# A mixture-of-experts decoder layer on one core: expert weights in six transfers of 2 MB per job instead of twelve of 1 MB

## What is computed

```python
logits = jnp.dot(hf, w_router) + b_router
top_v, top_e = lax.top_k(logits, TOP_K)            # TOP_K = 4
top_w = jax.nn.softmax(top_v, axis=-1)
...
def expert_block(args):                            # 128 rows of one expert
    xb, e = args
    gu = xb @ w_gate_up[e] + b_gate_up[e]          # w_gate_up[e]: 1024 x 2048
    gate = jnp.minimum(gu[:, 0::2], SWIGLU_LIMIT)
    up = jnp.clip(gu[:, 1::2], -SWIGLU_LIMIT, SWIGLU_LIMIT)
    act = (up + 1.0) * gate * jax.nn.sigmoid(SWIGLU_ALPHA * gate)
    return act @ w_down[e] + b_down[e]             # w_down[e]: 1024 x 1024
```

## Time and profile before

| | before |
|---|---|
| median of 3 runs | 2044.56 us |
| the profiled execution | 2048.57 us, of which the span 2046.5 us |
| TensorE (PE) busy | 1911.9 us, 93% of the span |
| VectorE (DVE) busy | 1455.7 us, 71% |
| ScalarE (ACT) busy | 1105.6 us, 54% |
| GpSimd (POOL) busy | 363.6 us, 18% |
| moved by DMA | 500.21 MB in 247399 packets |
| loads of gate-up / down pieces | 262 / 128, 1024.0 KB each |

### The profile page before, as it was taken

How to read it: one execution, slowest core, us unless ns; L and a number is a source line. 1 busy time by engine, 2 the same in 40 slices (tenths; PEclk the granted TensorE clock), 3 DMA queues, 4 the chain that set the end, 5 groups by cost and what they waited for, 6 DMA issues and landing times.

```text
span 2046.5 us, 27803 instructions
## 1 busy us (share of the span) xinstructions
PE 1911.9 (93%) x9552; PEld 1487.8 (73%) x9552; DVE 1455.7 (71%) x1677; ACT 1105.6 (54%) x1203; POOL 363.6 (18%) x260
## 2 busy tenths in 40 slices
PE   6899899975899986599999999999999999999998
PEld 2444699943756886488888888888888888888884
DVE  4517544344522454599999999999999999999995
ACT  2014222215541221277777777777777777777771
POOL 2000333302000000022222131222212121222211
PEclk9999999977799997599999999999999999999998
DMA  9820000003003221599999999999999999999996
GB/s 349 314 74 1 0 1 2 1 1 149 1 1 123 83 83 55 198 368 364 371 366 372 366 371 369 363 371 368 367 366 371 370 369 369 371 369 364 371 364 245
DMA packets 247399, 500.21 MB, mean 244 GB/s; under 512 B 14730, under 2 KB 16839, under 8 KB 246131
## 3 DMA queue, kind: packets, MB, share of 16 engines
q1 hardware_dynamic: 235108, 480.87, 64.8%
q0 software_dynamic: 9648, 17.32, 2.3%
q10 hardware_dynamic: 2592, 1.31, 0.2%
HBM read 495.76 MB, written 21.51 MB: 253 GB/s over the span
## 4 chain that ended last, share of the span: by engine, by line
PE 58%; DVE 0%; ACT 0%; ACTq 0%; issue 0%
PE bank L1836 17%; PE bank L1834 17%; PE bank L1835 17%; PE bank L1831 1%; PE bank L1849 1%; PE bank L1821 1%; PE bank L1912 1%; PE bank L1906 0%; DVE sb_e_lo L2032 0%; ACT sb_e_hi L1918 0%; DVE sb_mod L2120 0%; DVE sb_mod L2123 0%; DVE sb_x L2125 0%; ACTq L1767 0%; DVE sb_x_lo L2029 0%; ACT sb_y L1928 0%
## 5 line engine op out<-in xcount | busy, mean ns | idle before, releaser
L2032 DVE TENSOR_TENSOR sb_e_lo<-sb_w_raw,sb_e_hi 128x2048 fp32r<-128x2048 f32 x388 | 875.2, 2282 | 1.8 <-ACT sb_e_hi L1918 1.8
L1918 ACT CAST sb_e_hi<-sb_w_raw 128x2048 fp32r<-128x2048 f32 x389 | 742.6, 1909 | 82.2 <-PE bank L1836 49.0
L1834 PE MATMUL bank<-sb_e_hi,sb_x_hi 128*128 128x512 f32 x1032 | 409.7, 397 | 0.0
L1836 PE MATMUL bank<-sb_e_hi,sb_x_lo 128*128 128x512 f32 x1032 | 404.4, 392 | 0.0
L1835 PE MATMUL bank<-sb_e_lo,sb_x_hi 128*128 128x512 f32 x1032 | 403.5, 391 | 0.0
L2003 POOL TENSOR_TENSOR sb_tick<-sb_ones 128x1 f32<-128x1 f32 x64 | 138.5, 2163 | 877.3 <-DVE sb_row L2101 696.9
L1836 PEld LDWEIGHTS bank<-sb_e_hi,sb_x_lo 128*128 128x128 f32 x1032 | 194.3, 188 | 42.6
L1835 PEld LDWEIGHTS bank<-sb_e_lo,sb_x_hi 128*128 128x128 f32 x1032 | 194.6, 189 | 40.3
L1834 PEld LDWEIGHTS bank<-sb_e_hi,sb_x_hi 128*128 128x128 f32 x1032 | 194.8, 189 | 36.6
L1834 PE MATMUL bank<-sb_e_hi,sb_a_hi 128*128 128x512 f32 x512 | 205.5, 401 | 0.0
L1836 PE MATMUL bank<-sb_e_hi,sb_a_lo 128*128 128x512 f32 x512 | 200.3, 391 | 0.0
(11 more groups left out here) (389 smaller groups left out, 2743.7 us busy)
## 6 DMA issues: line engine op xcount, KB each, us to landing
sb_w_raw<-in_w_gate_up_dram SPq DMA_DIRECT2D x262, 1024.0 KB, 7.0
sb_w_raw<-in_w_down_dram SPq DMA_DIRECT2D x128, 1024.0 KB, 7.4
sb_ring<-in_ada_w_dram SPq DMA_DIRECT2D x12, 2048.0 KB, 12.7
sb_ring<-in_w_in_dram SPq DMA_DIRECT2D x7, 2048.0 KB, 9.9
sb_x<-in_x_dram SPq DMA_DIRECT2D x2, 2048.0 KB, 13.0
sb_ring<-in_w_out_dram SPq DMA_DIRECT2D x2, 2048.0 KB, 7.9
sb_e_hi<-y_rows SPq DMA_DIRECT2D x4, 1024.0 KB, 8.3
sb_e_lo<-y_rows SPq DMA_DIRECT2D x4, 1024.0 KB, 16.5
```

The source lines that it names most:

```text
L1834: te.matmul(out, hi[:, k0 + k, :], w_hi, start=(first and k == 0 and what >= 2 * GU), stop=False)
L1836: mm = te.matmul(out, lo[:, k0 + k, :], w_hi, start=False, stop=(last and k == 3))
L1918: return sc.copy(g.e_hi[:, p % PARTS, :, :], raw(p))
L2032: return ve.tensor_tensor(g.e_lo[:, p % PARTS, :, :], raw(p), g.e_hi[:, p % PARTS, :, :].bitcast(F32), ALU.subtract).then_inc(split_done[p ...
```

## The change

The two pieces that stand at positions 2i and 2i + 1 come in one transfer of 2 MB into two neighbouring places of `w_raw`, so that a job has six transfers. A gate-up pair is 1024 rows by 512 columns (runs of 2 KB in the source); a down pair is 512 rows by 1024 columns (runs of 4 KB). In the down pair the two pieces alternate in the partition's memory, so the views that ScalarE and VectorE read have four runs of 512 numbers with a gap of 512 between them. There are three semaphores `raw_in`, one for each pair of places. A pair is issued after the split of its second position. In routing, six loads of 1 MB become three of 2 MB.

```diff
-def raw_slot(g, p):
-    return g.w_raw[:, p % RAW, :].rearrange("p (k n) -> p k n", k=4)
+def raw_pair(g, p):
+    at = p % RAW // 2 * 2
+    return g.w_raw[:, at:at + 2, :].rearrange("p a n -> p (a n)")
+
+def raw_slot(g, p, what):
+    if what < 2 * GU:
+        return raw_pair(g, p).rearrange("p (h k n) -> p h k n", h=2, k=4)[:, what % 2]
+    return raw_pair(g, p).rearrange("p (k h n) -> p k h n", h=2, k=4)[:, :, what % 2]
+
+def load_pair(g, sp, p, what, e):
+    if what < 2 * GU:
+        src, k = g.a["w_gate_up"][0][bass.ds(e, 1), :, 256 * what:256 * what + 512], KD
     else:
-        half, n, w = (what - 2 * GU) // 2, what % 2, g.a["w_down"]
-    src = w[0][bass.ds(e, 1), 512 * half:512 * half + 512, 512 * n:512 * n + 512]
-    sp.dma_start(raw_slot(g, p), src.rearrange("a (k p) n -> p (a k) n", p=P)).then_inc(g.raw_in[p % RAW], 16)
+        half = (what - 2 * GU) // 2
+        src, k = g.a["w_down"][0][bass.ds(e, 1), 512 * half:512 * half + 512, :], 4
+    sp.dma_start(raw_pair(g, p).rearrange("p (k n) -> p k n", k=k), src.rearrange("a (k p) n -> p (a k) n", p=P)).then_inc(g.raw_in[p % RAW // 2], 16)
...
-            for i, p in enumerate(FIRST):
-                load_weights(g, sp, p, i, first)
-            for p in range(4):
-                load_weights(g, sp, p, CHUNK_AT[p], first)
+            load_pair(g, sp, FIRST[0], 0, first)
+            for p in (0, 2):
+                load_pair(g, sp, p, CHUNK_AT[p], first)
...
         def loaded(p, turn):
-            return raw_in[p % RAW], 32 * turn + (16 if p < 4 else 32 if p < 10 else 48)
+            return raw_in[p % RAW // 2], 32 * turn + (16 if p < 4 else 32 if p < 10 else 48)
...
-                for p in range(4, N_POS):
-                    sp.wait_ge(*(is_split(p - RAW, turn) if p >= RAW else is_split_before(p - RAW + N_POS, turn)))
-                    load_weights(g, sp, p, CHUNK_AT[p], after if p in (8, 9) else e)
-                for p in range(4):
-                    sp.wait_ge(*is_split(p - RAW + N_POS, turn))
-                    load_weights(g, sp, p, CHUNK_AT[p], after)
+                for p in range(4, N_POS, 2):
+                    sp.wait_ge(*(is_split(p + 1 - RAW, turn) if p >= RAW else is_split_before(p + 1 - RAW + N_POS, turn)))
+                    load_pair(g, sp, p, CHUNK_AT[p], after if p == 8 else e)
+                for p in (0, 2):
+                    sp.wait_ge(*is_split(p + 1 - RAW + N_POS, turn))
+                    load_pair(g, sp, p, CHUNK_AT[p], after)
```

More of the change, by code:

```diff
@@ L1467 @@
 PE_BACK = 3
-def raw_slot(g, p):
-    return g.w_raw[:, p % RAW, :].rearrange("p (k n) -> p k n", k=4)
-def load_weights(g, sp, p, what, e):
-    if what < 2 * GU:
-        half, n, w = what % 2, what // 2, g.a["w_gate_up"]
-    else:
-        half, n, w = (what - 2 * GU) // 2, what % 2, g.a["w_down"]
-    src = w[0][bass.ds(e, 1), 512 * half:512 * half + 512, 512 * n:512 * n + 512]
-    sp.dma_start(raw_slot(g, p), src.rearrange("a (k p) n -> p (a k) n", p=P)).then_inc(g.raw_in[p % RAW], 16)
-CHUNK_AT = list(range(2, 10)) + [0, 1, 10, 11]
+CHUNK_AT = list(range(2, 10)) + [0, 1, 10, 11]
+def raw_pair(g, p):
+    at = p % RAW // 2 * 2
+    return g.w_raw[:, at:at + 2, :].rearrange("p a n -> p (a n)")
+def raw_slot(g, p, what):
+    if what < 2 * GU:
+        return raw_pair(g, p).rearrange("p (h k n) -> p h k n", h=2, k=4)[:, what % 2]
[3 more added lines that the diff above has]
+        src, k = g.a["w_gate_up"][0][bass.ds(e, 1), :, 256 * what:256 * what + 512], KD
+    else:
+        half = (what - 2 * GU) // 2
+        src, k = g.a["w_down"][0][bass.ds(e, 1), 512 * half:512 * half + 512, :], 4
+    sp.dma_start(raw_pair(g, p).rearrange("p (k n) -> p k n", k=k), src.rearrange("a (k p) n -> p (a k) n", p=P)).then_inc(g.raw_in[p % RAW // 2], 16)
 def gather_rows(g, po, at):
@@ L1767, in job_count, with raw @@
             return eng.value_load(g.table[0:1, 0:1], min_val=MIN_JOBS, max_val=MAX_JOBS)
-        def raw(p):
-            return raw_slot(g, p)
+        def raw(p, what=None):
+            return raw_slot(g, p, CHUNK_AT[p] if what is None else what)
         def loaded(p, turn):
-            return raw_in[p % RAW], 32 * turn + (16 if p < 4 else 32 if p < 10 else 48)
+            return raw_in[p % RAW // 2], 32 * turn + (16 if p < 4 else 32 if p < 10 else 48)
         def is_split(p, turn):
@@ L1916, in _, with hi_part @@
         def _(sc):
-            def hi_part(p):
-                return sc.copy(g.e_hi[:, p % PARTS, :, :], raw(p))
+            def hi_part(p, what=None):
+                return sc.copy(g.e_hi[:, p % PARTS, :, :], raw(p, what))
             def features_hi(i, bank):
@@ L1931, in _ @@
             for i, p in enumerate(FIRST):
-                sc.wait_ge(raw_in[p % RAW], 16)
-                hi_part(p).then_inc(*first_act(f"g{i}"))
+                sc.wait_ge(raw_in[p % RAW // 2], 16)
+                hi_part(p, i).then_inc(*first_act(f"g{i}"))
                 sc.wait_ge(*first_pe.at(f"xt{i}"))
@@ L1936, in _ @@
             for p in range(3):
-                sc.wait_ge(raw_in[p], 16)
+                sc.wait_ge(raw_in[p // 2], 16)
                 if p == 2:
@@ L2029, in features_lo, with split @@
                 return ve.tensor_tensor(g.x_lo[:, at, :], ps[bank][:, :].rearrange("p (k n) -> p k n", k=4), g.x_hi[:, at, :].bitcast(F32), ALU.subtract)
-            def split(p):
-                return ve.tensor_tensor(g.e_lo[:, p % PARTS, :, :], raw(p), g.e_hi[:, p % PARTS, :, :].bitcast(F32), ALU.subtract).then_inc(split_done[p % PARTS], 1)
+            def split(p, what=None):
+                return ve.tensor_tensor(g.e_lo[:, p % PARTS, :, :], raw(p, what), g.e_hi[:, p % PARTS, :, :].bitcast(F32), ALU.subtract).then_inc(split_done[p % PARTS], 1)
             def ups(n):
@@ L2049, in _ @@
                 ve.wait_ge(*first_act.at(f"g{i}"))
-                split(p)
+                split(p, i)
                 ve.wait_ge(*first_act.at(f"xh{i}"))
@@ L2169, in decoder_layer @@
                 diag=([P, NT, PE_BACK, P], F32))
-            g.raw_in = [g.sem(moe, f"raw_in{i}") for i in range(RAW)]
+            g.raw_in = [g.sem(moe, f"raw_in{i}") for i in range(RAW // 2)]
             g.h2_out = g.sem(moe, "h2_out")
```

## The result

| | before | after |
|---|---|---|
| median of 4 runs | 2044.65 us | 2066.07 us (2061.32 to 2068.38) |
| ratio, 95% interval | | 1.0101 (1.0080 to 1.0122) |
| span of the profiled execution | 2046.5 us | 2061.9 us |
| job of the expert stage, mean of 31 | 35.59 us | 36.13 us (35.58 to 36.65) |
| first cast of the expert stage | 853.42 us | 851.68 us |

The forecast was no change. Of the two profiled executions, the span's 15.4 us are the stage's start, 1.7 us earlier, and 31 x 0.54 = 16.8 us in the jobs. The mean of a job is taken between the transposes of the next block's features (line 1828 after, 1821 before) that stand 31 jobs apart: 1120.01 us after, 1103.18 us before.

What follows compares the result with a forecast made beforehand. TensorE, busy 35.59 of 35.59 us a job, was taken as the bound. Span 2046.5 + 0 x 32 + 0 = 2046.5 us, 2048.6 us with 2.1 around it, 4.0 above the median: forecast 2044.6 us, range 2041.0 to 2049.6 us.

Steps and rivals of the forecast that it cites:

- What bounds the kernel: Expert stage: TensorE's matrix work sets the job, 35.59 us, and a faster weight stream can buy nothing.
- The landing of a pair: Weight loads: 2 MB alone land 7.8 us after issue, 2.4 us fixed plus 5.4 us of transfer.
- That slack is all but gone: Casts of the expert stage: time in hand before them nearly vanishes, and some wait up to 0.7 us.
- the term for POOL's rows: Gather and scatter of a job: each moves 0.27 MB and takes 0.7 us of the stream.
- The landing of (6,7): Last pair in the queue's round: lands at 1444.7 to 1446.1 us, 0.7 us early to 0.7 late for its cast.
- Nor does it pile up: Expert stage: late casts don't accumulate over jobs; under about a microsecond late, the split stays where it is.
- The spare time of the stream: Weight stream: needs 373 GB/s and runs at 389 when it has work, 1.5 us a job spare.
- Rival A: Expert stage, slower: late pair transfers starve TensorE in each job, +32 us at 1 us a job; chance 0.08.
- from a landing of 10.8 us on: Pair (0,1): if its transfer takes longer than about 10.8 us, the product of position 0 waits in each job.
- The cover of 3.4 us for position 6: Cast of position 6: may start at 1448.8 us, 3.4 us late, before TensorE's product has to wait.
- The start: Before the first cast: nothing waits for the first pair; no change, bounds 2.8 us less and 2.7 us more.
- The signs of being wrong: Profile after: TensorE waits for e_lo in steady jobs, landings past 10 us, or any change in job length.

Runs made afterwards that it cites:

- the gather runs: Kernel before with one more gather a job, 2046.46 us, or three more, 2123.88 us; changed kernel gathering 16 of 128 rows, 2047.62 us.
- late issue alone: Kernel before, still twelve 1 MB transfers, but both of a pair issued after the split of its second position; each cast waits for its own: 2047.38 us.
- holding alone: Kernel before, 1 MB transfers issued as before, but the cast of an even position waits until both of the pair have landed: 2046.43 us.
- eight places: Changed kernel with eight raw places instead of six, so pairs (0,1) and (6,7) no longer share: 2059.60 us, ratio 1.0063.

## Why the prediction was wrong

- **What bounds the kernel** was right. TensorE's 35.59 us a job stand as the floor: no run here has a shorter mean, and relieving the stream of most of the gather bought nothing below it.
- **The landing of a pair**, 2.4 + 5.4 = 7.8 us when the queue is short, was right: 7.9 us for (0,1) in the rows above, 8.0 us the median of the gate-up pairs. "That slack is all but gone" was right too.
- **The step that failed first is the term for POOL's rows**, 0.27 MB and "0.7 us of the stream" each. It measured 1.4 and 1.6 us in the landings, and 1.3 us by the run with three more gathers. Bytes at the weights' rate was no upper bound, and I gave it no other. The sum had this term at no cost to a job; with fewer rows gathered the whole loss is gone. The landing of (6,7), put at 9.2 us at most, is 10.9, and its cast waits 2.5 to 2.8 us instead of 0.7.
- **The step that let it through is "Nor does it pile up".** I held each pair's landing against today's issue and cast once, and called a late cast harmless while TensorE's product was not reached. But the late split is the next issue of the same places. The cycle adds up from rows that I had: casts to next issues 1436.94 - 1428.27 = 8.7 and 1420.00 - (1445.38 - 35.59) = 10.2 us, with my landings of 7.8 and at most 9.2 us 35.9 us, over 35.59. That would have been a warning and no proof, for the first two can shrink: they are 8.3 and 8.8 us in the changed kernel, and with these my landings give 34.1 us, which fits. What fills the cycle is the landing of (6,7), 10.9 us instead of 9.2.
- **The spare time of the stream** was put at 1.5 us a job. That is near what the gather runs give, 1.8 us, but I did not hold against it the dry spells that the late issues of whole pairs bring, 1.1 us twice in the job above.
- **Rival A**, starvation, came nearest: late landings recur in each job and the job grows. It had a chance of 0.08 and a price of 1 us a job; the job grew by 0.54 us. Its threshold, "from a landing of 10.8 us on", did not decide. It was worked out for pair (0,1), which lands after 7.9 us as forecast; that (6,7) lands after 10.9 us is no confirmation of it, since for (6,7) the prediction's own cover reached to 1448.8 - 1436.94 = 11.9 us. TensorE waits at the down products and not at that of position 0. The cover of 3.4 us for position 6 was used up, since the lateness of its cast came round through the next issues.
- **The start** lies within its bounds (2.8 us less to 2.7 more): 1.7 us less. That is no effect of the change that could be told: with the start unchanged the first cast came at 849.61 us (late issue alone) and at 854.61 us (holding alone). Packets (216,000 forecast, 211,511 measured), 195 issues and the hidden start of the first pair were as forecast. The signs of being wrong all came: TensorE waits for e_lo, down pairs land after 11.1 us, the job has changed its length. The cast waits were to be under 1 us and below 40 us in sum; they are up to 3.1 us, and 269 us.
- **The Trainium skill's sentence** that only the full count tells of all data, from "DMA: Bandwidth & Descriptors", section on why a DMA increments its semaphore by 16, is not tested here, but what it makes a pair do is priced: holding the first megabyte costs nothing alone and, with the late issue, 1.4%. The Trainium skill's tip that going from 2 KB to 4 KB can improve throughput a lot, from "Perfetto Trace Analysis", section DMA Optimizations, has the sign right: the 4 KB runs of a third of the weights give back 9 us. In a kernel of 2077 us that is 0.4%.

What stays open: why a lot of rows costs the stream about twice its bytes and twice its packets' own time, how the loss divides in the kernels with only some pieces in pairs, and whether the shared places or the dry spells of any late whole pair weigh more, since eight places brought back only a third.

## What to carry to other kernels

Before coarsening a transfer, add up the whole cycle of a buffer (landing, use, release, next issue) over a job and compare it with the job; a window held against each landing by itself misses that lateness comes round again. Count everything that shares the queue at a measured time, not at its bytes, and charge a dry spell wherever an issue comes less than the fixed part of a landing (2.4 us here) before the queue is empty. If loads are hidden by a few per cent, two changes that each cost nothing can cost 1.4% together.

## What was not expected of the hardware

A gather or scatter of about 0.27 MB in rows of 4 KB takes 1.3 to 1.6 us from a stream in which 2.1 MB of weights take 5.2 us; by its bytes it would be 0.7 us, and its packets took 0.70 us of the 16 engines' time. Weights in runs of 4 KB instead of 2 KB, a third of all, gave 9 us back in 2077, with the same number and size of transfers. From 1 MB to 2 MB the size itself gave nothing: 1.0140 and 1.0146 with the same issues and waits.
